# Second mixer's small levels and diagonal on four 32-column tiles of TensorE instead of two of 64

## What is computed

```python
def gla_scan(q, k, v, la, S0):          # la: log decay per token, head and key channel
    def step(Sst, inp):                 # one chunk
        Bc = jnp.cumsum(lac, axis=1)
        diff = Bc[:, :, None] - Bc[:, None, :]
        decay = jnp.exp(jnp.where(tril, diff, -jnp.inf))
        A = jnp.einsum('bthd,bshd,btshd->btsh', qc, kc, decay)
        o = jnp.einsum('btsh,bshv->bthv', A, vc) + jnp.einsum('bthd,bhdv->bthv', qc * jnp.exp(Bc), Sst)
        S_new = jnp.exp(Bc[:, -1])[..., None] * Sst + (k * exp(Bc[:, -1] - Bc))^T v
```

## Time and profile before

| | |
|---|---|
| median of 3 runs | 1217.97 us (1217.97 to 1220.23) |
| the profiled execution | 1219.62 us, its span 1216.4 us |
| PE busy | 1185.4 us (97%) |
| PEld busy | 1144.4 us (94%) |
| DVE busy | 747.1 us (61%), 1429 instructions |
| ACT busy | 389.1 us (32%), 523 instructions |
| mean granted TensorE clock | 0.991 |
| second mixer's prompt chunks | 285 to 431 us of the span |

### The profile page before, as it was taken

One profiled execution on the slowest core, in us unless ns is written; L12 is line 12 of the kernel. 1 busy time (PEld: TensorE's weight loads), 2 busy tenths in 40 slices (PEclk: granted clock), 3 DMA queues, 4 the chain that ended last, 5 costly groups with the idle time before them and its releaser, 6 DMA issues.

```text
span 1216.4 us, 21918 instructions
## 1 busy us (share of the span) xinstructions
PE 1185.4 (97%) x9289; PEld 1144.4 (94%) x9289; DVE 747.1 (61%) x1429; ACT 389.1 (32%) x523; POOL 2.3 (0%) x7
## 2 busy tenths in 40 slices
PE   8999999999999999999999999999999999999996
PEld 7999989889899998898999999999999999999995
DVE  6743566767878866555555667666666653323766
ACT  6232234323443432213343222222222321111533
POOL 0000000000000000000000000000000000000000
PEclk8999999999999999999999999999999999999998
DMA  6233111623233165654442542212122133223222
GB/s 214 74 136 106 70 41 64 191 101 94 100 99 115 65 223 182 211 182 144 155 144 90 182 159 85 78 70 105 70 75 99 59 135 128 70 91 96 100 70 78
DMA packets 48769, 138.44 MB, mean 114 GB/s; under 512 B 5364, under 2 KB 24948, under 8 KB 39584
## 3 DMA queue, kind: packets, MB, share of 16 engines
q1 hardware_dynamic: 16296, 89.39, 21.5%
q10 hardware_dynamic: 32376, 47.66, 11.4%
HBM read 113.15 MB, written 23.81 MB: 113 GB/s over the span
## 4 chain that ended last, share of the span: by engine, by line
PE 86%; DVE 5%; issue 4%; ACT 2%; DMA 1%; ACTq 1%; POOL 0%; DVEq 0%; POOLq 0%
PE ps L718 59%; PE ps L724 9%; PE ps L827 5%; PE ps L833 3%; PE ps L745 1%; PE aux L1015 1%; PE aux L972 1%; DMA xT<-in_xT 1%; PE aux L1031 1%; ACT whi L1759 1%; PE aux L935 1%; PE aux L962 1%; PE aux L929 1%; DVE wlo L1076 1%; PE aux L1025 0%
## 5 line engine op out<-in xcount | busy, mean ns | idle before, releaser
L718 PE MATMUL ps<-ahi,whi 128*128 128x288 f32 x1536 | 332.3, 298 | 1.8 <-issue 1.8
L718 PE MATMUL ps<-alo,whi 128*128 128x288 f32 x1536 | 329.9, 296 | 0.0
L718 PEld LDWEIGHTS ps<-ahi,whi 128*128 128x128 f32 x1536 | 248.1, 189 | 7.2 <-issue 4.4
L718 PEld LDWEIGHTS ps<-alo,whi 128*128 128x128 f32 x1536 | 246.0, 188 | 0.0
L1076 DVE TENSOR_TENSOR wlo<-wraw,whi 128x2048 fp32r<-128x2048 f32 (+1 forms) x87 | 187.5, 2155 | 89.4 <-ACT whi L1759 84.9
L1759 ACT ACTIVATE whi<-wraw 128x2048 fp32r<-128x2048 f32 (+1 forms) x87 | 156.4, 1798 | 147.6 <-PE ps L718 102.5
L718 PE MATMUL ps<-ahi,wlo 128*128 128x288 f32 x800 | 171.2, 296 | 0.0
L718 PEld LDWEIGHTS ps<-ahi,wlo 128*128 128x128 f32 x800 | 128.8, 189 | 0.0
L724 PE MATMUL ps<-ahi,wlo 128*128 128x288 f32 x736 | 105.4, 295 | 0.0
L724 PEld LDWEIGHTS ps<-ahi,wlo 128*128 128x128 f32 x736 | 100.5, 189 | 0.0
L718 PE MATMUL ps<-achi,whi 128*128 128x288 f32 x336 | 72.0, 296 | 0.0
(11 more groups left out here) (376 smaller groups left out, 1707.3 us busy)
## 6 DMA issues: line engine op xcount, KB each, us to landing
wraw<-in_w_in SPq DMA_DIRECT2D x31, 1024.0 KB, 5.0
wraw<-in_w_up SPq DMA_DIRECT2D x21, 1024.0 KB, 4.8
gate_scratch<-stg ACTq DMA_DIRECT2D x32, 288.0 KB, 3.5
gt<-gate_scratch ACTq DMA_DIRECT2D x32, 288.0 KB, 3.0
wraw<-in_w_pgate SPq DMA_DIRECT2D x6, 1024.0 KB, 4.8
wraw<-in_w_down SPq DMA_DIRECT2D x8, 704.0 KB, 4.0
wraw<-in_w_down SPq DMA_DIRECT2D x8, 640.0 KB, 3.9
out_C_s<-st ACTq DMA_DIRECT2D x16, 256.0 KB, 2.9
```

What stands on the lines that cost most here:

```text
L718: mm = nc.tensor.matmul(ps[:, t % 2, a, 0:HALF], w, x(k)[:, a * HALF:(a + 1) * HALF], start=f, stop=e)
```

## The change

The diagonal and the levels 16, 8, 4, 2 and 1 are computed by four groups of 32 tokens, each with itself: four matmuls a head with 32 stationary columns and 32 (diagonal) or 16 (levels) moving ones, whose results go to PSUM partitions 0, 32, 64 and 96. Level 32, which lies between two such groups, keeps its two matmuls a head; its result is no longer merged into `attd` under a mask but copied straight into `att`, two blocks of 32 by 32 a head, in two DVE copies. `attd` and the masks have 32 columns a head instead of 64. The masks `cmaskq` are made at c = 0 from `cmask` by four copies, `att` is then cleared as a whole, and ACT copies four blocks of `attd` onto the diagonal of `att` instead of two. The sample's stages stay as they were.

```diff
--- before.py
+++ after.py
@@ -35,6 +35,7 @@
 TS = NB * LS
 T = TP + TS
 HALF = T // 2
+QT = 32
 H = 4
 DK, DV = 128, 256
 L = 128
@@ -264,7 +265,8 @@
         cmask = put("cmask", [P, 8, P // 2], I8)
         NMASK = where[0]
         nmask = put("nmask", [P, 2, P])
-        attd = at("attd", [P, H, P // 2], F32, NMASK)
+        attd = at("attd", [P, H, QT], F32, NMASK)
+        cmaskq = at("cmaskq", [P, 8, QT], I8, NMASK + 4 * H * QT)
         bmask = put("bmask", [P, 4])
         gains = put("gains", [P, 6, KT])
         convw = put("convw", [P, 3, FT])
@@ -548,6 +550,9 @@
 
         def half_of(e):
             return slice(TS * e, TS * (e + 1))
+
+        def quarter_of(e):
+            return slice(QT * e, QT * (e + 1))
 
         h_out_of, tn_need, copied, norms = {}, {}, 0, 0
         for s in sched:
@@ -986,10 +991,14 @@
                         pe.wait_ge(fm_ready, 4 * H)
                     b = bank(j)
                     for h in range(H):
-                        for e in range(2) if c < NC else (h % 2,):
-                            at_, t1 = (h * TS, t0 + TS * e) if c < NC else (h // 2 * TS, t0)
-                            mm = nc.tensor.matmul(b[half_of(e), at_:at_ + TS], gk[:, h, t1:t1 + TS],
-                                                  gq[:, h, t1:t1 + TS], start=True, stop=True)
+                        for e in range(4) if c < NC else ():
+                            t1 = t0 + QT * e
+                            mm = nc.tensor.matmul(b[quarter_of(e), h * QT:(h + 1) * QT], gk[:, h, t1:t1 + QT],
+                                                  gq[:, h, t1:t1 + QT], start=True, stop=True)
+                        if c == NC:
+                            at_ = h // 2 * TS
+                            mm = nc.tensor.matmul(b[half_of(h % 2), at_:at_ + TS], gk[:, h, t0:t0 + TS],
+                                                  gq[:, h, t0:t0 + TS], start=True, stop=True)
                     mm.then_inc(aux_ready, 1)
                     pe.wait_ge(kf_ready, c + 1)
                     b = bank(j + 1)
@@ -1008,6 +1017,13 @@
                             if w == TS:
                                 mm = nc.tensor.matmul(b[0:TS, h * TS:(h + 1) * TS], xl[:, h, 0:TS], xl[:, h, TS:],
                                                       start=True, stop=True)
+                                continue
+                            if c < NC and w < QT:
+                                for e in range(4):
+                                    late = xl[:, h, quarter_of(e)].rearrange("p (b s) -> p b s", s=2 * w)[:, :, w:]
+                                    mm = nc.tensor.matmul(b[quarter_of(e), h * QT // 2:(h + 1) * QT // 2]
+                                                          .rearrange("p (b s) -> p b s", s=w),
+                                                          xl[:, h, quarter_of(e)], late, start=True, stop=True)
                                 continue
                             for e in range(2) if c < NC else (h % 2,):
                                 at_, r = (h * TS // 2, half_of(e)) if c < NC else (h // 2 * TS // 2, half_of(0))
@@ -1563,7 +1579,10 @@
                     if c:
                         dve.wait_ge(gat_ready, c)
                     else:
-                        V.memset(att[TS:, :, 0:TS], 0.0)
+                        V.memset(att[:, :, :], 0.0)
+                        for e in range(4):
+                            V.tensor_copy(cmaskq[quarter_of(e), :, :],
+                                          cmask[quarter_of(e), :, QT * (e % 2):QT * (e % 2 + 1)])
                     link(V.memset(attd[:, :, :] if c < NC else att[:, :, :], 0.0))
 
                     for h in range(H):
@@ -1604,8 +1623,8 @@
 
                     b = job(j)
                     if c < NC:
-                        i = V.copy_predicated(attd[:, :, :], bcast(cmask[:, 7, :], H, 1),
-                                              b[:, 0:H * TS].rearrange("p (h s) -> p h s", h=H))
+                        i = V.copy_predicated(attd[:, :, :], bcast(cmaskq[:, 7, :], H, 1),
+                                              b[:, 0:H * QT].rearrange("p (h s) -> p h s", h=H))
                     else:
                         for e in range(2):
                             r = half_of(e)
@@ -1634,9 +1653,14 @@
                             return x.rearrange("p h (b s) -> p h b s", s=2 * w)[:, :, :, w:]
                         if w == TS:
                             i = V.tensor_copy(att[0:TS, :, TS:], b[0:TS, 0:H * TS].rearrange("p (h s) -> p h s", h=H))
+                        elif c < NC and w == QT:
+                            for e in range(2):
+                                r = slice(TS * e, TS * e + QT)
+                                i = V.tensor_copy(att[r, :, TS * e + QT:TS * (e + 1)],
+                                                  b[r, 0:H * QT].rearrange("p (h s) -> p h s", h=H))
                         elif c < NC:
-                            i = V.copy_predicated(late(attd[:, :, :]), late(bcast(cmask[:, k, :], H, 1)),
-                                                  b[:, 0:H * TS // 2].rearrange("p (h b s) -> p h b s", h=H, s=w))
+                            i = V.copy_predicated(late(attd[:, :, :]), late(bcast(cmaskq[:, k, :], H, 1)),
+                                                  b[:, 0:H * QT // 2].rearrange("p (h b s) -> p h b s", h=H, s=w))
                         else:
                             for e in range(2):
                                 r = half_of(e)
@@ -2059,8 +2083,8 @@
                         A.activation(x[:, :, :, w:], x[:, :, :, w:], ACT.Exp, scale=1 / TAU).then_inc(xl_exp, 1)
                 elif s[0] == "lev" and s[1] < NC and s[2] == 3:
                     act.wait_ge(attd_ready, s[1] + 1)
-                    for e in range(2):
-                        i = A.activation(att[half_of(e), :, half_of(e)], attd[half_of(e), :, :], ACT.Copy)
+                    for e in range(4):
+                        i = A.activation(att[quarter_of(e), :, quarter_of(e)], attd[quarter_of(e), :, :], ACT.Copy)
                     i.then_inc(gat_ready, 1)
                 elif s[0] == "gout":
                     c = s[1]
```

## The result

The changed kernel takes **1223.69 us** (median of 6 runs, 1221.93 to 1225.07), where the kernel before takes 1219.72 in its 6 runs beside it (1217.97 to 1220.66). The ratio is 1.0034, with a 95% interval of 1.0021 to 1.0047: 4 us slower, where 0.9 us slower was forecast. The profiled execution took 1223.86 us (before: 1219.62), its span is 1221.8 us (1216.4), and the mean granted clock of TensorE was 0.985 (0.991).

A forecast was written before the change was run, and what follows sets the result against it. PE, busy 97% of the span, was taken as the bound; chunk 0 at +1.5 us and chunks 1 to 3 at -0.6 gave +0.9 on the median 1217.97, so 1218.9 us, range 1215.4 to 1221.8.

The forecast's parts named there:

- PE's part: Diagonal and small levels on four tiles: 0.2 us saved a group, 1.2 a chunk, 4.8 in all if PE were everything.
- Rival 2: Small groups on PE: four tiles don't start fast enough, 24 groups cost 11.3 us, kernel at 1228; chance 1 in 10.
- DVE's and ACT's parts: Copies in the second mixer: chunk 0's mask copies +1.1 us, level 32 up to +0.25, ACT's four diagonal copies +0.43 a chunk.
- Chunk 0's sum: Late DVE and ACT make att ready 1.5 us later in chunk 0, PE already waiting for it: +1.5 us.
- Chunks 1 to 3, -0.2 us each: att ready 0.5 + 0.14 - 0.43 = 0.2 us earlier, PE waiting a microsecond for it; -0.6 us for the three.
- the gain of the last masked copy: DVE's last masked copy of a chunk, 0.44 us long, was to get 0.14 us shorter.
- The base: The starting time to which +0.9 us was added: the median of the runs before, 1217.97 us.
- Rival 1, the clock: After chunk 0's wait before level 64, PE runs at half speed some 3.5 us: +0.8 us, 1219.7; chance 0.28.
- Its cover: DVE's delay after level 64 in chunk 0 was to hide about 0.9 of the 1.7 us PE loses at half clock.
- Rival 3, faster: Copies in the chunks are not the bound: cheaper or overlapping copies give 1216.5, DVE also moving ahead 1215; chance 0.14.
- PE's four shorter groups are all spent in waits: In chunk 0, PE's saving on four groups brings no time, since PE waits for DVE and ACT anyway.

The follow-up runs named there:

- the pair with mask copies: Kernel before plus four DVE copies of the mask copies' size, without and with 8 idle matmuls on PE before level 64: ratios 1.0025 and 1.0007.
- level 64's wait filled: Changed kernel plus 9 idle matmuls on PE before level 64 of chunk 0: 1223.41 us, ratio 1.0028 to the kernel before.
- the filled kernel: Changed kernel plus idle matmuls in four PE waits (level 64, two in gout of chunk 0, the sample's state): 1221.60 us, ratio 1.0014.
- the kernel with early masks: Changed kernel with the four mask copies moved ahead into a DVE wait at the last value tile: 1222.98 us, ratio 1.0021 to the kernel before.
- the kernel before with mask copies: Kernel before plus four DVE copies of the mask copies' size, nothing else changed: 1222.85 us, ratio 1.0025.
- the one with all three edits: Changed kernel with mask copies moved ahead, two of ACT's four copies on GpSimd, last level before the tile's evacuation: 1219.57 us, ratio 0.9993.

## Why the prediction was wrong

**PE's part: right.** The group of 32 products was forecast at 0.47 us, and takes 0.45; a round of four at 32 ns, and takes 36. The 1.2 us a chunk that it saves are there, as counted above. Rival 2, four tiles that don't start fast enough, is refuted. So is, for products on different column tiles, the start-to-start of 25 ns that the Trainium skill gives (page "TensorE: Matmul & The Clock Gate", section "Wait — 56ns, not 53.3ns?"): the products here follow each other every 9 ns on average. The row with which the prediction had argued against that rule, two products begun within 40 ns, doesn't decide it, since 25 ns fit in; a narrower window of the same trace does:

```profile
293.46 0.25 PE L1015 MATMUL aux<-xl 128*64 128x32 f32 x2
```

This is PE from 293.45 to 293.47 us, so the two began within 10 ns.

**DVE's and ACT's parts: right.** Mask copies 269 ns each (forecast 290), 1.12 us in all; level 32's two copies 0.58 us (0.59); masked copies of levels 250 ns (272); ACT's four copies 1.26 us (1.27 forecast, where 4 x 0.315 is 1.26).

**Chunk 0's sum, +1.5 us: nearly right as a path.** The wait before level 64 is 2.30 us (2.3 to 2.5 forecast). With the clock full the chunk is 1.74 us longer; the mask copies make 1.22 of it. As it runs, it is 3.51 longer.

**Chunks 1 to 3, -0.2 us each: a little off.** They came to -0.07, -0.12 and +0.05. PE waits 0.76 us for ACT in each, as forecast (1 us). What was mis-sized is the gain of the last masked copy: it was taken as 0.14 us from its length. Its length did shrink, 0.44 to 0.28 us, but ACT starts by its signal. From the start of the copy to the start of ACT it was 353.85 - 353.32 = 0.53 us; now, in the timeline of DVE and ACT after:

```profile
356.27 0.28 DVE L1662 COPY_PREDICATED attd<-cmaskq,aux 128x64 f32<-128x64 int8 x1
...
356.76 1.26 ACT L2087 ACTIVATE att<-attd 32x128 f32<-32x128 f32 x4 [4.07 <-DVEq L1673]
```

it is 0.49, a gain of 0.04. Together the path comes to about +1.6 us where +0.9 was forecast. That alone would have stayed within the range.

**The base: 1.75 us too low.** The forecast put its +0.9 on the median of three executions, 1217.97. Beside the changed kernel the kernel before took 1219.72, and its mean over 109 later executions is 1219.7. So of the 4.8 us between 1218.9 and 1223.69, 1.75 are not the change at all; the other 3.0 or so are what the forecast missed of it, some 0.7 on the path and 2.4 by the clock.

**Rival 1, the clock: the step that failed.** The forecast's sum put the clock at nothing, and that is what the runs contradict: about 2.4 of the 4.0 us are its. The mechanism was named as a rival, with a chance of 0.28 and at +0.8 us; it came true, and dearer, since its price and its reach were wrong, in three ways.
- *Its length.* It was priced with the 3.5 us half-clock stretch behind a wait of 1.8 us. The other row quoted beside it, 6.5 us of it behind 2.83, was the nearer one: behind 2.30 us it lasts 6.8.
- *Its cover.* DVE's lateness was to cover 0.9 of 1.7 us. But PE loses 2.8 us: 0.4 on level 32 (1.07 us for 0.66), and 2.4 on the large tile behind it (295.51 to 304.52, 9.01 us; before, from 294.04 to 300.63, 6.59). So DVE, instead of being waited for, waits 2.07 us for PE's tile. Chunk 0's part of the clock is 3.51 - 1.74 = 1.8 us, not 0.8; the pair with mask copies gives 1.95.
- *Its reach.* It was put at one place. The rest of PE's part was costed as if waits that the change makes cost their own length alone: gout's waits of chunk 0, and the four for ACT. With level 64's wait filled, the clock fell in gout instead, and filling four waits, not one, brought 2.4 of the 4.0 us back. All in all the clock accounts for about 2.4 to 2.6 us: by the filled kernel (2.4, with 1.9 either way), and by the slope over 109 executions, a correlation.

The sum is then 1.6 us for the path, which the filled kernel has in its four chunks (+1.57) and in its time (+1.6), and 2.4 for the clock, 4.0 together. That trace and time agree so closely is partly luck: in the filled kernel's profiled execution the state's stage is 0.7 us longer as well, and the stretch behind 621 us costs 1.5. "PE's four shorter groups are all spent in waits" was true on the path, and missed that a group that gets shorter inside a wait makes the wait longer.

**Rival 3, faster,** was right about where a gain lay, in the order of DVE's work, though not about which gap: not the 0.85 us for ACT's exp, but the tile's evacuation ahead of the last level. It needed an edit that the change didn't make.

What stays open: why the clock falls in one execution behind a given wait and not in another. The kernel before shows 1.98 us without a fall, the changed one 2.02 with one. Behind the same wait for `st` at 254 us, 1.98 us long, it fell in the kernel with early masks, and behind 1.99 us there it didn't in the kernel before with mask copies. Waits of 0.56, 1.14 and 0.76 us at the end of chunk 0 had no fall with early masks, where 0.59, 1.14 and 0.76 had one with level 64's wait filled. And behind a wait of 2.71 us, longer than the one before level 64, it stayed full in two kernels, the one with all three edits (at 1197 us) and the one with four filled waits (PE's timeline, then a window, clock 1.00):

```profile
1200.70 0.36 PE L759 MATMUL ps<-ehi,whi 128*128 128x256 f32 x1 [2.71 <-DVE sgp L1270]
...
1200.70:1204.20 3.50, 3.29 (x25) 3.09 (x26) 3.13 (x8) 0.94 (x3) 0.00 (x0) 1.00 0.04 14
```

So the length of a wait alone doesn't say whether the clock falls. The kernel with early masks has a low mean clock though its chunks hardly wait longer. The part of the clock that comes from outside the chunks is therefore counted, by mean clocks, but not explained wait by wait.

## What to carry to other kernels

In a kernel that TensorE bounds, work taken from it pays only where nothing else sets the end of that stage; otherwise it becomes idle time, and idle time can cost more than its own length, since matmuls behind it may run at half speed. An edit that shortens a wait doesn't always bring that back: with the masks early alone, the wait before level 64 was 0.9 us shorter and the kernel still 0.21% slower. Look at what the engine behind the shortened one must now do in time (here one masked copy and four small ACT copies), and make room for it first: with the masks made in a gap of DVE and the last level taken ahead of the tile's evacuation, the same narrower tiles are 0.14% faster than the kernel before (0.06 to 0.23%) instead of 0.34% slower. That is the better of two versions with the same gain in the chunks; the other, with GpSimd on top, is at 0.07%, with no change inside its interval. To see whether a wait costs by the clock, fill it with idle matmuls and leave all else alone, and judge by the mean clock of many executions, since one profile shows only one draw.

## What the runs showed of the hardware

- Products on four 32-column tiles, 32 stationary and 16 moving columns in 32 bits, follow each other every 9 ns on average (64 in 0.74 us, 32 in 0.45), where those of 64 columns on two tiles took 29.
- The lower clock was seen behind waits of PE of 1.3, 1.4, 1.6, 1.9, 2.0 and 2.3 us, and not seen behind others of 1.1, 1.4, 1.6, 1.9, 2.0 and even 2.71 us. Behind a wait of 2.29 or 2.30 us before level 64 it came in all three kernels profiled that had one.
- ACT's copies of 32 and of 64 partitions do not overlap one another (four in 1.26 us, 307 ns each), and GpSimd's copy of the same shape takes 289 ns: for so small a copy it was as good an engine as ACT, as far as the profile's rough spans of GpSimd tell.
- What the lower clock costs depends on what follows: at 249 us in the kernel before it took up 1.5 us that PE otherwise waits for `st` (0.47 us of waiting for 1.98), while behind that second wait, in the kernel with early masks, chunk 0 began 1.3 us later.
- A copy of 32x256 bytes takes DVE 269 ns, about what it takes for 32x128 elements of 32 bits (284 ns).
